# Quartered weight splits, a free pair of banks for the last turn, and moved pieces of work in a two-block transformer kernel

## Chip, core and metric

The kernel runs on one core of a Trainium2 chip. The metric is the device time of one execution in microseconds (us). Five engines work side by side, each through its own instructions in order: TensorE (PE in the profile), VectorE (DVE), ScalarE (ACT), GpSimd (POOL) and the DMA queue of SyncE (SP). They wait for each other by semaphores only.

## The reference, cut to what matters

512 positions of width 1024 go through two blocks of two layers each, all in float32.

```
first block, layer l:   x += rmsnorm(mixer_l(rmsnorm(x)))       mixer_0 = fox, mixer_1 = lru
                        x += rmsnorm(cross_attention(rmsnorm(x), rmsnorm(mem)))
                        x += rmsnorm(swiglu(rmsnorm(x)))
second block, layer l:  x = ln(a*x + 0.5*swiglu(x));  x = ln(a*x + nsa(x));  x = ln(a*x + 0.5*swiglu(x))

attention of one query tile:  s = q @ k.T + mask;  p = softmax(s);  o = p @ v;   y = concat(o) @ w_out
fox:   8 heads of 64, causal, half of the input of w_out is a gated convolution (y_b) without attention
cross: 4 heads of 256 over 256 memory rows
nsa:   8 heads of 96; three branches per head: compressed keys (31 of them), and two causal ones;
       a quarter of the input of w_out is a pooled branch (y_pool) without attention
```

## The kernel before, in words

**Weights.** Every weight matrix comes in units of up to 128x2048 numbers (a list `units`, in the order of use). A unit is loaded by SP into one of three staging buffers `STG`, cast by ACT to the matmul type into one of three `WR` buffers (`hi`, line 984), and DVE writes what the cast lost beside it (`lo`, line 1460). TensorE makes each product of three matmuls, high by high, high by low, low by high (`mm3`, lines 500 to 502). ACT and DVE have no scheduler: `after(name)` in their programs means "here cast the unit three places behind `name`". A cast waits until the buffer of the unit three places before it is dropped; a `lo` waits for its `hi`.

**Stages.** fox, cross (x0), feed-forward (f0), lru, cross (x1), f1, then f2, nsa (n0), f3, f4, nsa (n1), f5. The weight products fill most of the time. The attention of fox, x0, x1, n0 and n1 is one loop of steps, written once for each engine (`attend`) and driven by `att_steps`. An item is one or more heads of one query tile. Step i holds, in this order on TensorE: the scores of item i, the turning (transposes, `tr`, line 505) of the probabilities of item i-2, and their product with v for item i-3. DVE takes the maximum of the scores of item i (line 1567) and copies every other turned item out of PSUM (line 1480); ACT does the exponentials of item i (line 991) and the other copies (line 1071). When the last item of a query tile is through, DVE scales its output (`finish`), TensorE turns it (`turn_result`), and ACT and DVE split it into high and low parts in `HT` for the product with w_out (`ohi`, `olo`).

**Banks.** PSUM has eight banks. In fox scores go round banks 2 to 4 and turned items round 5 to 7; in cross and nsa scores go round 2 and 3, turned items and turned results round 4 and 5. The compressed scores of nsa take a bank of the same round as the scores. `pick` and `room` make TensorE wait until the former user of a bank is through. The product with w_out (`out_proj`) keeps query tile t in banks 2t and 2t+1.

**Order around the change.** `hook(i)` runs at the beginning of step i. In fox, hooks 1, 2, 5 and 6 split y_b (`ybs`: an ACT cast of 128x512, line 1183, and a DVE subtraction), hooks 4 and 8 split one whole weight unit each; in cross, hook 5 splits one; in nsa, hooks 12 and 20. In nsa the compressed branch of a query tile has four parts: `scores` (TensorE product, line 898; DVE mask and maximum; ACT exponential), `norm` (DVE), `turn` (TensorE, ACT), `out` (TensorE, line 915; DVE), placed by `nsa_hook`. The scores of the first query tile come ahead of step 0. In `out_proj` the list `first` gives the order of tiles in the first group of rows of w_out, with the last `turn_result` among them.

Of the kernel before, what the change touches and what calls it, by code (L numbers as in the profile page):

```python
# [15 lines left out]
NT = 4  # L16
# [185 lines left out]
def build(nc, T, out):  # L202
    with ExitStack() as ctx:
# [113 lines left out]
        FOX_YBS = {1: 2, 2: 3, 5: 0, 6: 1}  # L317
# [38 lines left out]
        t_banks = {"f": (5, 6, 7), "x": (4, 5), "n": (4, 5)}  # L356
        on_parts = {"f": (0, 4, F_ON), "x": (0, 8, X_ON), "n": (2, 6, N_ON)}
# [123 lines left out]
        def tensor(pe):  # L481
# [82 lines left out]

            def out_proj(s, nk, operand, points, first=range(NT), plain=False):

                names = down_units(s, nk)
                rows_of = [name[2] for name in names]
                groups = [[k] for k in rows_of[:-2]] + [rows_of[-2:]]
                for group in groups:  # L570
                    last_group = len(group) == 2
                    for t in first if group[0] == groups[0][0] else range(NT):
                        if callable(t):
                            t()
                            continue
                        if group[0] == groups[0][0]:
                            free = (ve, (s, "yfree", t)) if s in rms else (ac, (s, "sq", t))
                            room(2 * t, free)
                            room(2 * t + 1, free)
                        for k0 in group:  # L580
                            if k0 == nk - 2 and t >= 2 and not plain and s != "f5":
                                turn(s, t - 2)
                            w = take((s, "d", k0))
                            for j in range(2):
                                k = k0 + j
                                g.wait_ge(*points(k, t))
                                lh, ll = operand(k)
                                for half in range(2):
                                    c = slice(half * 512, half * 512 + 512)
                                    last = mm3(P[:, 2 * t + half, :], lh[:, tcol(t)], ll[:, tcol(t)], w[0][:, j, c],  # L590
                                               w[1][:, j, c], k == groups[0][0], k == groups[-1][-1] + 1)
                        if last_group:
                            last.then_inc(mm.sem, mm.up(s, "y", t))
                    if not last_group:
# [6 lines left out]
            def attend(s, need, values, hook=None):  # L601
# [56 lines left out]
                return lambda: turn_result(items[-1]["t"])  # L658
# [17 lines left out]
            def fox():  # L676
# [44 lines left out]
                for c in range(4):  # L721
                    w = take(("fox", "qk", c))
                    for j in range(2):
# [7 lines left out]
                         [1, 2, last_turn, 3, 0], plain=True)  # L731

            def cross(l):
# [34 lines left out]
                out_proj(s, 8, ht_operand, lambda k, t: ve.at(s, "olo", t, k // 4 * 4), [1, 0, last_turn, 2, 3])  # L768
# [41 lines left out]
            def nsa(l, prev):  # L810
# [121 lines left out]
                out_proj(s, 8, ht_operand, lambda k, t: ve.at(s, "yp", 1) if k < 2 else ve.at(s, "olo", t, 0 if k < 6 else 4),  # L932
                         [1, 3, last_turn, 2, 0])
# [42 lines left out]
        def scalar(a):  # L976
            g = Gate(a)

            def hi(n):
# [4 lines left out]
                a.copy(WR[0:p, n % NWR, 0, 0:k * w], STG[0:p, n % NSTG, 0:k * w]).then_inc(ac.sem, ac.up("hi", n))  # L984

            def after(name):
                if U[name] + 3 < len(units):
                    hi(U[name] + 3)
# [19 lines left out]
            def norm_tile(s, t, between=None, turned=None):  # L1008
# [36 lines left out]
            def down(s, nk, prepare=None, plain=False):  # L1045
# [6 lines left out]
                for t in range(NT):  # L1052
                    norm_tile(s, t, (lambda: after(names[-2])) if t == NT - 1 else None,
                              t - 1 if t in (1, 2) and not plain and s != "f5" else None)
                if plain:
                    after(names[-1])

            def attend(s, hook=None):
                items = items_of[s]()
                for i, it, b_, c_, ends in att_steps(s):  # L1060
# [22 lines left out]
                    for it in ends:  # L1083
# [3 lines left out]
                        for j0 in range(0, nk, 4):  # L1087
# [3 lines left out]
                            a.copy(HT[:, 0, k0 + j0:k0 + j0 + m, tcol(t)], ps).then_inc(ac.sem, ac.up(s, "ohi", t, j0))  # L1091

# [31 lines left out]
            def fox():  # L1124
# [51 lines left out]
                def hook(i):  # L1176
                    if i in (4, 8):
                        after(("fox", "qk", 2 if i == 4 else 3))
# [6 lines left out]
                attend("fox", hook)  # L1185
                down("fox", 8, plain=True)

            def cross(l):
# [17 lines left out]
                attend(s, lambda i: after((s, "q", 3)) if i == 5 else None)  # L1206
# [37 lines left out]
            def lru():  # L1244
# [80 lines left out]
                gates(2)  # L1325
                after(("lru", "ai", 2))
                gelu(0)
# [17 lines left out]
            def nsa(l, prev):  # L1345
# [80 lines left out]
                def hook(i):  # L1426
                    if i in (12, 20):
                        after((s, "v", 0 if i == 12 else 4))
                    for part, t in nsa_hook(i):
                        if part == "scores":  # L1430
                            scores(t)
                        if part == "turn":
                            cmp_turn(t)

                scores(ORDER["n"][0])
                attend(s, hook)
# [16 lines left out]
        def vector(v):  # L1453
            g = Gate(v)

            def lo(n):
                _, _, p, k, w = units[n]
                g.wait_ge(*ac.at("hi", n))
                cut = slice(0, k * w)
                v.tensor_tensor(WR[0:p, n % NWR, 1, cut], STG[0:p, n % NSTG, cut], WR[0:p, n % NWR, 0, cut].bitcast(F32),  # L1460
                                ALU.subtract).then_inc(ve.sem, ve.up("lo", n))

            def after(name):
                if U[name] + 3 < len(units):
                    lo(U[name] + 3)
# [34 lines left out]
            def norm_tile(s, t, between=None, turned=None):  # L1500
                if s in rms:
                    post, pre, n = rms[s]
                    if post:
# [12 lines left out]
                        if between and s not in ("fox", "lru"):  # L1516
                            between()
                    if pre:
# [25 lines left out]
            def down(s, nk, prepare=None, plain=False):  # L1544
# [6 lines left out]
                for t in range(NT):  # L1551
                    norm_tile(s, t, (lambda: after(names[-2])) if t == NT - 1 else None,
                              t - 1 if t in (1, 2) and not plain and s != "f5" else None)
                if plain:
                    after(names[-1])

            def attend(s, finish, hook=None):
                items = items_of[s]()
                for i, it, b_, c_, ends in att_steps(s):
# [10 lines left out]
                    if b_ and turned_by_vector(b_, i - 2):  # L1570
# [3 lines left out]
                        if j >= NP:  # L1574
                            g.wait_ge(*mm.at(s, "o", j - NP))
                        cp(PTB[j % NP][:, 0:kx], P[:, where[s, "t", j], 0:kx], s, "tc", j)
                    if c_ and c_["last"]:
                        finish(c_, i - 3)
                    for it in ends:
# [3 lines left out]
                        for j0 in range(0, nk, 4):  # L1583
# [4 lines left out]
                            rest(HT[:, 1, ks, tcol(t)], ps, HT[:, 0, ks, tcol(t)], s, "olo", t, j0)  # L1588

# [46 lines left out]
            def fox():  # L1636
# [61 lines left out]
                def hook(i):  # L1698
                    if i in (4, 8):
                        after(("fox", "qk", 2 if i == 4 else 3))  # L1700
# [18 lines left out]
                attend("fox", finish, hook)  # L1719
                down("fox", 8, plain=True)  # L1720

            def cross(l):
# [28 lines left out]
                attend(s, finish, lambda i: after((s, "q", 3)) if i == 5 else None)  # L1751
# [124 lines left out]
            def nsa(l, prev):  # L1876
# [152 lines left out]
                def hook(i):  # L2029
                    if i in (12, 20):  # L2030
                        after((s, "v", 0 if i == 12 else 4))
                    for part, t in nsa_hook(i):
# [4 lines left out]
                        if part == "out":  # L2037
                            cmp_out(t)

                scores(ORDER["n"][0])  # L2040
                attend(s, finish, hook)
# [70 lines left out]
```

## Time and profile before

| | |
|---|---|
| time, median of 3 runs (lowest to highest) | 3573.73 us (3573.02 to 3575.31) |
| the profiled execution: own time; span of its instructions | 3575.89 us; 3574.1 us |
| busy share of the span: PE, PEld (weight loads), DVE, ACT | 98%, 82%, 41%, 33% |
| mean granted TensorE clock, as a share of full speed | 0.994 |

The span runs from the first to the last instruction of the profiled execution; its own time is 1.8 us longer and lies 2.2 us above the median of the runs. Busy times of PE are modelled from pipelined matmuls, so what counts here is the idle time between them, with the engine and line that ended it.

### The profile page before, as it was taken

How to read it: one execution, taken by the hardware profiler on the slowest of the kernel's cores; microseconds unless marked ns; L12 is line 12 of the kernel's file. 1: busy time of each engine (PE TensorE's matmuls, PEld its weight loads, DVE VectorE, ACT ScalarE, POOL GpSimd, SP SyncE). 2: the span in 40 equal slices, each digit the busy share in tenths (PEclk: the TensorE clock that was granted, in tenths of full speed). 3: DMA queues.
4: the chain of work that ended last, by engine and by line, in shares of the span. 5: the costliest groups of instructions: out<-in, count | busy, mean ns of one | idle time of the engine just before them, and what ended most of it. 6: DMA issues, size and time to landing. Idle time of an engine off the chain costs nothing.

```text
span 3574.1 us, 39697 instructions
## 1 busy us (share of the span) xinstructions
PE 3493.7 (98%) x17605; PEld 2937.4 (82%) x17605; DVE 1460.0 (41%) x1538; ACT 1185.4 (33%) x1725; POOL 61.1 (2%) x68
## 2 busy tenths in 40 slices
PE   8999999999999999999999999999999999999999
PEld 7788788888787888888888778888888887788887
DVE  4444433337644323333335564223422345552333
ACT  3343332236633322232224343222322333432222
POOL 2000000000000000000000000000000000000000
PEclk9999999999999999999999999999999999999999
DMA  5214132223241322232322202332332223013221
GB/s 161 90 53 153 48 118 94 95 89 101 95 147 55 112 94 94 94 107 94 103 92 78 68 25 95 94 99 101 97 104 95 94 79 97 24 58 108 94 95 59
DMA packets 246333, 326.44 MB, mean 91 GB/s; under 512 B 18320, under 2 KB 215232, under 8 KB 246160
## 3 DMA queue, kind: packets, MB, share of 16 engines
q1 hardware_dynamic: 241232, 308.77, 26.7%
q0 software_dynamic: 4928, 15.12, 1.3%
q8 instruction: 138, 2.26, 0.3%
q14 instruction: 35, 0.29, 0.0%
HBM read 321.74 MB, written 2.10 MB: 91 GB/s over the span
## 4 chain that ended last, share of the span: by engine, by line
PE 89%; DVE 6%; ACT 4%; issue 0%; DMA 0%; SPq 0%; POOL 0%; DVEq 0%; ACTq 0%
PE P L500 27%; PE P L502 27%; PE P L501 27%; PE P L505 3%; PE P L653 3%; PE P L628 2%; DVE WR L1460 2%; DVE BIG L1468 1%; ACT WR L984 1%; ACT BIG L991 1%; DVE BIG L1477 1%; ACT XN L991 0%; DVE HT L1468 0%; DVE STAT L1567 0%; ACT BC L991 0%
## 5 line engine op out<-in xcount | busy, mean ns | idle before, releaser
L1460 DVE TENSOR_TENSOR WR<-STG,WR 128x2048 fp32r<-128x2048 f32 (+2 forms) x300 | 669.1, 2232 | 1356.8 <-ACT WR L984 1356.5
L500 PE MATMUL P<-HT,WR 128*128 128x512 f32 (+1 forms) x3016 | 1123.7, 373 | 5.9 <-DVE WR L1460 3.0
L501 PE MATMUL P<-HT,WR 128*128 128x512 f32 (+1 forms) x3016 | 1120.6, 372 | 0.0
L502 PE MATMUL P<-HT,WR 128*128 128x512 f32 (+1 forms) x3016 | 1120.4, 371 | 0.0
L984 ACT CAST WR<-STG 128x2048 fp32r<-128x2048 f32 (+2 forms) x300 | 557.4, 1859 | 1080.4 <-PE P L502 1080.2
L500 PEld LDWEIGHTS P<-HT,WR 128*128 128x128 f32 x3016 | 569.5, 189 | 105.0 <-DVE WR L1460 4.3
L502 PEld LDWEIGHTS P<-HT,WR 128*128 128x128 f32 x3016 | 569.4, 189 | 98.1
L501 PEld LDWEIGHTS P<-HT,WR 128*128 128x128 f32 x3016 | 569.4, 189 | 96.9
L500 PE MATMUL P<-WR,HT 128*128 128x512 f32 (+1 forms) x1344 | 525.3, 391 | 12.3 <-DVE HT L1468 12.3
L502 PE MATMUL P<-WR,HT 128*128 128x512 f32 (+1 forms) x1344 | 521.9, 388 | 0.0
L501 PE MATMUL P<-WR,HT 128*128 128x512 f32 (+1 forms) x1344 | 521.5, 388 | 0.0
L500 PEld LDWEIGHTS P<-WR,HT 128*128 128x128 f32 x1344 | 253.4, 189 | 63.1 <-DVE HT L1468 9.0
L502 PEld LDWEIGHTS P<-WR,HT 128*128 128x128 f32 x1344 | 253.0, 188 | 50.6
L501 PEld LDWEIGHTS P<-WR,HT 128*128 128x128 f32 x1344 | 253.5, 189 | 49.6
L991 ACT ACTIVATE XN<-P 128x512 f32<-128x512 f32 (+1 forms) x160 | 103.6, 651 | 554.6 <-PE P L502 554.5
L1477 DVE SCALAR_TENSOR_TENSOR BIG<-XN,P 128x512 f32<-128x512 f32 x132 | 90.7, 687 | 341.5 <-PE P L502 341.5
L628 PE MATMUL P<-BIG 128*128 128x256 f32 (+3 forms) x448 | 149.9, 441 | 7.1 <-ACT BC L991 6.8
L653 PE MATMUL P<-BIG,XN 128*128 128x96 f32 (+2 forms) x928 | 141.9, 294 | 6.2 <-DVE XN L1480 5.9
L991 ACT ACTIVATE BC<-P,STAT 128x256 f32<-128x256 f32 (+3 forms) x192 | 98.9, 520 | 109.0 <-DVE STAT L1567 108.7
L653 PEld LDWEIGHTS P<-BIG,XN 128*128 128x128 f32 x928 | 124.5, 198 | 10.1 <-DVE XN L1480 7.1
L500 PE MATMUL P<-WR,RB 128*128 128x512 f32 (+1 forms) x384 | 122.3, 334 | 0.0
L1567 DVE TENSOR_REDUCE STAT<-P 128x1 f32<-128x512 f32 (+4 forms) x142 | 83.4, 590 | 94.3 <-PE P L632 66.0
(178 smaller groups left out, 2369.6 us busy)
## 6 DMA issues: line engine op xcount, KB each, us to landing
STG<-in_w_ffn_gu_dram SPq DMA_DIRECT2D x44, 1024.0 KB, 5.1
STG<-in_ffn_w_gate_dram SPq DMA_DIRECT2D x44, 1024.0 KB, 5.3
STG<-in_ffn_w_up_dram SPq DMA_DIRECT2D x44, 1024.0 KB, 5.3
STG<-in_ffn_w_down_dram SPq DMA_DIRECT2D x44, 1024.0 KB, 4.9
STG<-in_w_ffn_down_dram SPq DMA_DIRECT2D x22, 1024.0 KB, 4.8
STG<-in_w_xkv_dram SPq DMA_DIRECT2D x16, 1024.0 KB, 5.4
STG<-in_w_in_dram SPq DMA_DIRECT2D x12, 1024.0 KB, 5.2
STG<-in_w_xq_dram SPq DMA_DIRECT2D x8, 1024.0 KB, 5.2
```

What stands on the lines that cost most here:

```text
L500: pe.matmul(o, lh, rh, start=first, stop=False)
L501: pe.matmul(o, lh, rl, start=False, stop=False)
L502: return pe.matmul(o, ll, rh, start=False, stop=last)
L505: return pe.transpose(o, i, IDENT[0:n, 0:n])
L628: last = pe.matmul(P[:, b, n * kx:(n + 1) * kx], l, r, start=j == 0, stop=j == len(qk) - 1 and a["diag"] is None)
L653: last = pe.matmul(o, PTB[j0 % NP][:, c:c + 128], c_["v"][n][j], start=j == 0, stop=j == nj - 1)
L984: a.copy(WR[0:p, n % NWR, 0, 0:k * w], STG[0:p, n % NSTG, 0:k * w]).then_inc(ac.sem, ac.up("hi", n))
L991: a.activation(o, i, f, **kw).then_inc(ac.sem, ac.up(*point))
L1460: v.tensor_tensor(WR[0:p, n % NWR, 1, cut], STG[0:p, n % NSTG, cut], WR[0:p, n % NWR, 0, cut].bitcast(F32), ALU.subtract).then_inc(ve.sem, ...
L1468: v.tensor_tensor(o, x, y, op).then_inc(ve.sem, ve.up(*point))
L1477: v.scalar_tensor_tensor(out=o, in0=x, scalar=s, in1=y, op0=op0, op1=op1).then_inc(ve.sem, ve.up(*point))
L1567: v.tensor_reduce(STAT[:, 80 + h:80 + h + nh], P[:, where[s, "s", i], 0:nh * kx].rearrange("p (h n) -> p h n", h=nh), AX.X, ALU.max, negat ...
```

## The change

- **Splits in quarters.** `hi` and `lo` can do a quarter of a unit. The whole units of hooks 4 and 8 (fox), 5 (cross), 12 and 20 (nsa) become four quarters each, at the ends of the steps listed in `SPLITS`.
- **y_b splits** of fox go to the ends of steps 3 to 6.
- **The last `turn_result`** goes to fixed banks (`last_banks`: accumulators that are free by then) and one tile product earlier in `first`.
- **nsa:** the first tile's product with the first rows of w_out (tile 3, whose operand is y_pool) goes ahead of the second to last step; the compressed scores of the first tile go from before step 0 into step 2, those of the next from step 7 to 9, and DVE's and ACT's part of all compressed scores, and DVE's `norm`, go from the beginning of a step to its end; a small product (`second(1)`) goes behind a 24-matmul one.
- **Other places:** in fox DVE copies v out of PSUM before a split instead of after it; at the end of fox and lru the last weight split goes ahead of the last tile's second norm (`middle`); in lru two gelus go ahead of a cast.

The diff, cut:

```diff
-        FOX_YBS = {1: 2, 2: 3, 5: 0, 6: 1}
+        FOX_YBS = {3: 2, 4: 3, 5: 0, 6: 1}
+        SPLITS = {"f": {7: (("qk", 2), 0), 8: (("qk", 2), 1), 9: (("qk", 2), 2), 11: (("qk", 2), 3), 12: (("qk", 3), 0),
+                        13: (("qk", 3), 1), 14: (("qk", 3), 2), 15: (("qk", 3), 3)},
+                  "x": {3: (("q", 3), 0), 4: (("q", 3), 1), 5: (("q", 3), 2), 7: (("q", 3), 3)},
+                  "n": {9: (("v", 0), 0), 10: (("v", 0), 1), 11: (("v", 0), 2), 12: (("v", 0), 3), 27: (("v", 4), 0),
+                        28: (("v", 4), 1), 29: (("v", 4), 2), 30: (("v", 4), 3)}}
+        last_banks = {"f": (1,), "x": (6, 7), "n": (0, 1)}
-            parts = {"norm": (1, 8, 24, 38), "turn": (3, 16, 32, 40), "out": (5, 20, 36, 44), "scores": (None, 7, 23, 37)}
+            parts = {"scores": (2, 9, 23, 37), "norm": (3, 10, 24, 38), "turn": (5, 16, 32, 40), "out": (7, 20, 36, 44)}
...
-                def turn_result(t):
+                def turn_result(t, banks=None):
-                        b = pick(tbank, (ve, (s, "olo", t, j0)))
+                        b = room(banks[j0 // 4], (ve, (s, "olo", t, j0))) if banks else pick(tbank, (ve, (s, "olo", t, j0)))
...
-                return lambda: turn_result(items[-1]["t"])
+                return lambda: turn_result(items[-1]["t"], last_banks[s[0]])
...
-                         [1, 2, last_turn, 3, 0], plain=True)          # fox
+                         [1, last_turn, 2, 3, 0], plain=True)
-                out_proj(... "x" ..., [1, 0, last_turn, 2, 3])
+                out_proj(... "x" ..., [1, last_turn, 0, 2, 3])
-                second(1)
                 head("k", 1, 0, "k", ve)
                 drop((s, "k", 1))
+                second(1)
...
-                scores(ORDER["n"][0])
+                    if i == len(nsa_items()) + 1:                       # in nsa's hook on TensorE
+                        out_tile(s, 8, ht_operand, points, 3, 0)
-                out_proj(s, 8, ..., [1, 3, last_turn, 2, 0])
+                out_proj(s, 8, ht_operand, points, [1, last_turn, 2, 0])
...                                                                   # scalar
+            def split_part(s, i):
+                if i in SPLITS[s[0]]:
+                    name, part = SPLITS[s[0]][i]
+                    after((s, *name), part, 4)
+                    if middle:                                          # norm_tile, between the two norms
+                        middle()
-                if plain:
-                    after(names[-1])
+                              (lambda: after(names[-1])) if plain and t == NT - 1 else None)
...
+                    split_part(s, i)                                    # end of each step of attend
+                    if tail:
+                        tail(i)
...
                 gates(2)
+                gelu(0)
                 after(("lru", "ai", 2))
-                gelu(0)
                 gelu(1)
...                                                                   # vector
+                        if s == "fox" and j == 3:
+                            g.wait_ge(*ve.at("fox", "ybs", 3))
-                after(("fox", "v", 0))
                 for t in range(NT):
                     g.wait_ge(*mm.at("fox", "v", 4))
                     cp(F_V[:, t, :], P[:, where["fox", "v", t], :], "fox", "v", t)
+                after(("fox", "v", 0))
...
-                second(1)
                 after((s, "k", 0))
                 key(2)
+                second(1)
```

## Rows read from the trace of the kernel before

**Rows 1.** The page: busy time of each engine, its share of the span, instructions.

```profile
PE 3493.7 (98%) x17605; PEld 2937.4 (82%) x17605; DVE 1460.0 (41%) x1538; ACT 1185.4 (33%) x1725; POOL 61.1 (2%) x68
```

**Rows 2.** PE's waits: for whom, us in total, times, longest.

```profile
PE P L505 <- DVE HT L1468: 14.3, 6, 3.7
PE P L500 <- DVE HT L1468: 13.9, 7, 4.4
...
PE P L628 <- ACT BC L991: 6.8, 6, 2.1
PE P L653 <- DVE XN L1480: 5.9, 5, 1.8
PE P L849 <- DVE FX L1480: 4.1, 2, 2.1
...
PE P L505 <- ACT BC L991: 2.2, 2, 1.2
```

**Rows 3.** PE's timeline: start, us, instruction, [idle before <- what ended it].

```profile
118.80 0.50 PE L500 MATMUL P<-HT,WR 128*128 128x512 f32 x1 [1.17 <-DVE BIG L1480]
...
224.43 0.50 PE L500 MATMUL P<-WR,HT 128*128 128x512 f32 x1 [1.40 <-DVE HT L1468]
...
276.80 0.58 PE L500 MATMUL P<-RB,WR 128*128 128x256 f32 x1 [2.31 <-DVE WR L1460]
...
405.20 0.47 PE L500 MATMUL P<-WR,HT 128*128 128x512 f32 x1 [1.65 <-DVE HT L1468]
...
897.74 0.77 PE L500 MATMUL P<-RB,WR 128*128 128x512 f32 x1 [3.47 <-DVE BIG L1468]
...
932.96 0.76 PE L500 MATMUL P<-WR,HT 128*128 128x512 f32 x1 [4.40 <-DVE HT L1468]
...
2024.91 1.90 PE L898 MATMUL P<-FX,BIG 96*128 96x31 f32 x16
...
2068.65 0.90 PE L505 MATMUL P<-CST,BC 128*128 128x128 f32 x3 [3.74 <-DVE HT L1468]
...
2132.73 0.66 PE L505 MATMUL P<-CST,BC 128*128 128x128 f32 x4 [2.44 <-DVE HT L1468]
...
2144.55 0.47 PE L500 MATMUL P<-WR,HT 128*128 128x512 f32 x1 [1.61 <-DVE HT L1468]
```

**Rows 4.** PE in short stretches: length, busy time, granted clock, DMA.

```profile
177.60:181.00 3.40, 1.96 (x12) 0.99 0.71 248
181.00:184.30 3.30, 3.30 (x16) 0.50 0.00 0
...
2998.90:3002.30 3.40, 1.41 (x8) 1.00 0.02 5
```

**Rows 5.** Single steps: length, then busy PE, PEld, DVE, ACT, POOL; clock.

```profile
171.96:174.31 2.35, 2.35 (x18) 1.72 (x17) 1.45 (x1) 1.35 (x2) 0.00 (x0) 1.00 0.00 0
...
366.99:368.94 1.95, 1.95 (x12) 1.61 (x10) 1.04 (x1) 0.88 (x1) 0.00 (x0) 1.00 0.00 0
...
2076.43:2078.14 1.71, 1.71 (x15) 1.35 (x13) 1.61 (x6) 1.31 (x4) 0.00 (x0) 1.00 0.00 0
```

**Rows 6.** DVE's timeline: fox steps 0, 1 and 4, n0 step 7.

```profile
163.57 0.69 DVE L1567 TENSOR_REDUCE STAT<-P 128x1 f32<-128x512 f32 x1 [0.22 <-PE P L632]
...
166.23 0.68 DVE L1567 TENSOR_REDUCE STAT<-P 128x1 f32<-128x512 f32 x1
...
172.86 2.29 DVE L1460 TENSOR_TENSOR WR<-STG,WR 128x2048 fp32r<-128x2048 f32 x1 [2.11 <-ACT WR L984]
...
2026.84 0.42 DVE L1468 TENSOR_TENSOR BIG<-P,CST 128x248 f32<-128x248 f32 x1 [2.35 <-PE P L898]
```

**Rows 7.** ACT's timeline: fox steps 1 and 4, the cast ahead of lru's gelus.

```profile
164.98 0.61 ACT L1183 CAST HT<-XN 128x512 fp32r<-128x512 f32 x1
...
170.93 1.89 ACT L984 CAST WR<-STG 128x2048 fp32r<-128x2048 f32 x1
...
893.77 1.91 ACT L984 CAST WR<-STG 128x2048 fp32r<-128x2048 f32 x1
```

More of the change, by code:

```diff
@@ L563, in first_feats, with out_groups, out_tile @@
                             drop(name)
-            def out_proj(s, nk, operand, points, first=range(NT), plain=False):
[L567 to L572, printed above, removed]
+            def out_groups(s, nk):
+                rows_of = [name[2] for name in down_units(s, nk)]
+                return [[k] for k in rows_of[:-2]] + [rows_of[-2:]]
+            def out_tile(s, nk, operand, points, t, n, plain=False):
+                groups = out_groups(s, nk)
+                if n == 0:
+                    free = (ve, (s, "yfree", t)) if s in rms else (ac, (s, "sq", t))
+                    room(2 * t, free)
+                    room(2 * t + 1, free)
+                for k0 in groups[n]:
+                    if k0 == nk - 2 and t >= 2 and not plain and s != "f5":
+                        turn(s, t - 2)
+                    w = take((s, "d", k0))
+                    for j in range(2):
+                        k = k0 + j
+                        g.wait_ge(*points(k, t))
+                        lh, ll = operand(k)
+                        for half in range(2):
+                            c = slice(half * 512, half * 512 + 512)
+                            last = mm3(P[:, 2 * t + half, :], lh[:, tcol(t)], ll[:, tcol(t)], w[0][:, j, c],
+                                       w[1][:, j, c], k == groups[0][0], k == groups[-1][-1] + 1)
+                return last
+            def out_proj(s, nk, operand, points, first=range(NT), plain=False):
+                groups = out_groups(s, nk)
+                for n, group in enumerate(groups):
+                    for t in first if n == 0 else range(NT):
                         if callable(t):
@@ L575, in out_proj @@
                             continue
[L576 to L592, printed above, removed]
+                        last = out_tile(s, nk, operand, points, t, n, plain)
+                        if n == len(groups) - 1:
                             last.then_inc(mm.sem, mm.up(s, "y", t))
-                    if not last_group:
+                    if n < len(groups) - 1:
                         last.then_inc(mm.sem, mm.up(s, "group", group[0]))
@@ L1006, in turn, with norm_tile @@
                     a.copy(HT[:, 0, ks, tcol(t)], ps).then_inc(ac.sem, ac.up(s, "hi", t, half))
-            def norm_tile(s, t, between=None, turned=None):
+            def norm_tile(s, t, between=None, turned=None, middle=None):
                 if s in rms:
@@ L1174, in fox, with tail @@
                         after(("fox", "qk", c))
-                def hook(i):
-                    if i in (4, 8):
-                        after(("fox", "qk", 2 if i == 4 else 3))
+                def tail(i):
                     if i in FOX_YBS:
@@ L1426, in hook, with tail @@
                 def hook(i):
-                    if i in (12, 20):
-                        after((s, "v", 0 if i == 12 else 4))
+                    for part, t in nsa_hook(i):
+                        if part == "turn":
+                            cmp_turn(t)
+                def tail(i):
                     for part, t in nsa_hook(i):
@@ L1498, in scaled, with norm_tile @@
                 stt(norm_buf[t % rms[s][2]], X[:, t, :], STAT[:, 8 + t:9 + t], BC[:, 1, :], ALU.mult, ALU.mult, s, "xn", t)
-            def norm_tile(s, t, between=None, turned=None):
+            def norm_tile(s, t, between=None, turned=None, middle=None):
                 if s in rms:
@@ L1517, in norm_tile @@
                             between()
+                    if middle:
+                        middle()
                     if pre:
@@ L1552, in down, with attend @@
                     norm_tile(s, t, (lambda: after(names[-2])) if t == NT - 1 else None,
[L1553 to L1557, printed above, removed]
+                              t - 1 if t in (1, 2) and not plain and s != "f5" else None,
+                              (lambda: after(names[-1])) if plain and t == NT - 1 else None)
+            def attend(s, finish, hook=None, tail=None):
                 items = items_of[s]()
@@ L1696, in fox, with tail @@
                         after(("fox", "qk", c))
-                def hook(i):
-                    if i in (4, 8):
-                        after(("fox", "qk", 2 if i == 4 else 3))
+                def tail(i):
                     if i in FOX_YBS:
@@ L1717, in finish @@
                     ve.name("fox", "on", "x", t)
-                attend("fox", finish, hook)
+                attend("fox", finish, tail=tail)
                 down("fox", 8, plain=True)
@@ L1749, in finish @@
                     ve.name(s, "on", "x", t)
-                attend(s, finish, lambda i: after((s, "q", 3)) if i == 5 else None)
+                attend(s, finish)
                 down(s, 8)
@@ L2029, in hook, with tail @@
                 def hook(i):
-                    if i in (12, 20):
-                        after((s, "v", 0 if i == 12 else 4))
+                    for part, t in nsa_hook(i):
+                        if part == "out":
+                            cmp_out(t)
+                def tail(i):
                     for part, t in nsa_hook(i):
@@ L2036, in hook @@
                             cmp_norm(t)
[L2037 to L2041, printed above, removed]
+                attend(s, finish, hook, tail)
                 down(s, 8)
```

47 lines of the change are left out of this document (26 added, 21 removed).

## The prediction

> **What bounds the kernel.** I read the page's busy times first, then PE's waits, then PE's timeline at each wait, and at last the timelines of DVE and ACT there. TensorE is busy for 3493.7 of 3574.1 us; DVE and ACT are busy for 41% and 33% [rows 1]. So the change can gain only what TensorE stands idle or runs slowly, and DVE and ACT matter only where they come late. The waits come in pairs because x0 and x1, and n0 and n1, are the same code [rows 2]. In the timeline each is one stall of 1 to 4.4 us at a known place [rows 3].
>
> There is a second loss. After the stall that ends at 179.04 TensorE had been busy for 1.96 of 3.40 us; in the next 3.30 us the granted clock is 0.50, the 1.2 GHz level, and sixteen instructions fill the stretch [rows 4]. At the 2.4 GHz level they would take half, so such a stretch costs 1.65 us. Of such stretches at 0.50, nine lie behind stalls that the change touches (one in fox, one each behind the stalls of 2.31 us at the ends of fox and lru, four in n0, two in n1). The same stall of 2.06 us was followed by 0.50 in n0 and by 1.00 in n1 [rows 2, 4], so the clock is not certain to follow.
>
> **What goes away.** Sum by the groups of [rows 2]; the parts that stay are named.
> - Scores and transposes behind the splitting of a result (14.3 us): 3.74 and 2.44 in each nsa [rows 3] go; 0.96 in each cross stays, its code is untouched. 12.4 us. In n0 the 3.74 arises because DVE waits for the cast of a whole unit, then subtracts 2.29 us, and only then comes to the result. The 2.44 is filled by the moved product of tile 3, which waits for nothing of the last attention tile.
> - First group of w_out (13.9 us): 1.40 in fox, 1.65 in x0 and x1, 1.61 and 1.60 in n0 and n1 [rows 3], 7.9 in all. There the turned last tile sits in a bank that the next tile product needs. In free banks it has one to two more products of twelve matmuls as cover. The 4.40 us of lru and 1.6 us at the start stay.
> - Scores behind an exponential (6.8 us): 1.13 and 2.12 in each nsa, 6.5 us; 0.16 in each cross stays.
> - Products behind a DVE copy (5.9 us): 1.77 in fox [rows 2], 1.81 in each cross, some 0.27 in each nsa. All behind whole units or y_b splits.
> - `second(1)` (4.1 us): 24 matmuls now lie ahead of it; what it waits for is there 2 us after the old place. Transposes behind an exponential in fox (2.2 us) go as well.
> - The last weight of fox and lru (2.31 each, 4.6 us): its ACT cast stood behind the second norm. In `middle` both halves fit while ACT would wait for DVE, and the norm that comes 0.6 us later is wanted only three products on.
> - v of fox: four copies now stand ahead of a subtraction of 2.29 us, 1.17 us [rows 3].
> - lru: the gelus go ahead of a cast of 1.91 us [rows 7], on whose other side TensorE waits 3.47 us for their bank [rows 3]. But the next stall, 4.40 us ahead of w_out, is the end of ACT's and DVE's own chain, which has the same work as before. Only ACT's own waits for TensorE in between are saved. Bounds 0 and 3.47; I take 1.5.
>
> Stalls: 12.4 + 7.9 + 6.5 + 5.9 + 4.1 + 2.2 + 4.6 + 1.2 + 1.5 = 46.3 us. With nine slow stretches of 1.65 us, 61.2 us.
>
> **What comes anew.** A quarter is a cast of 128x512 on ACT and a subtraction of 128x512 on DVE. The y_b splits have just these shapes: the cast takes 0.61 us [rows 7], and from one maximum on DVE to the next, with the exponential, the cast and the subtraction between them, pass 2.66 us [rows 6]. This loop is the price, for both engines take their work in order: the cast stands behind the exponential, which waits for the maximum, and DVE's next maximum stands behind the subtraction. TensorE's step takes 2.35 us with 512 columns in fox, 1.95 in cross, 1.71 with 384 columns [rows 5]. With fewer columns the maximum and the exponential shorten; estimates from the 0.69 us of 512 columns are 2.4 us for 384 and 2.2 for 256.
> - Cross: four quarters, each 0.2 us late; 0.8 us is less than the step or so between a copy and its use. Nothing.
> - Fox: steps 3 to 7 lose 0.3 us each (y_b splits and the first quarter), seven steps with 384 columns 0.7 each: 6.4 us late. A copy may be 1.8 us late, and step 10, which has no quarter, makes up 1.1. 3.5 us of stalls in steps 8 to 16.
> - nsa, start: TensorE now does two scores, then the compressed scores need the bank of the first: a stall of 2.0 us, for DVE's maximum stands behind the y_pool subtraction. Step 3 then waits 0.65 us for the masked scores. 2.65.
> - nsa, step 10: the compressed scores share two banks with the scores, and DVE's mask addition (the 0.42 us instruction [rows 6] that today starts right behind the product of 1.90 us [rows 3]) moves behind the maximum, the copy and a quarter of step 9. From the end of scores 9: maximum 0.65, exponential 0.8, cast 0.5, subtraction 0.7, addition 0.4, together 3.1 us; TensorE has a turning and a product, 1.3 us. It waits 1.8 us.
> - nsa, steps 10 to 12: `finish` and `norm` and quarters stand in one queue on DVE; the next copies are 1.55 and 0.65 us late. 2.2.
> - nsa, steps 27 to 30: the loop of 2.4 against 1.71 us, right behind a `finish`: 0.7 late four times, and 0.3 us was already missing there. The copies come 1.05 and 2.0 us late. 3.05.
> - nsa, steps 23 and 37: the same bank wait as in step 10 without a quarter, 0.4 each; `norm` of the last tile, now behind `finish`, makes its turning 1.15 later. 1.95.
> - nsa, end: the moved product waits 0.8 us for banks 6 and 7, which `finish` of the branch before reads; step 21 still waits 0.4 us for the result's split. 1.2.
>
> So nsa pays 12.9 us each time, fox 3.5, together 29.3. Each of these is an estimate from the rows named; its bounds are nothing (the delay fits into the step behind) and twice as much.
>
> The quarters' casts end later than the whole units did, and the loads behind them start later; the units behind are wanted only in the product with w_out or the next stage, over 50 us on, and no wait for a DMA stands in [rows 2].
>
> **A rule against a row.** The loop of 2.66 us [rows 6] says that quarters stall too. The Trainium skill, Perfetto Trace Analysis, section Optimizing Scalar/DVE Operations, says that where these engines are not saturated but cause bubbles elsewhere, breaking up instructions may let work be completed sooner; taken alone it gives the sum without the new stalls. The same section says that each instruction carries a fixed cost, some 60 ns on DVE and 93 ns on ScalarE from SBUF, so grouping helps a saturated engine: for 24 more pairs, 3.7 us as an estimate, were none hidden. No row shows a whole unit and four quarters side by side.
>
> **Sum.** 61.2 - 29.3 = 31.9 us less. The profiled execution took 3575.9 us, so 3544.0 us; the median of the runs shown is 2.2 us lower: 3542 us, 0.9% faster. Its own range is 3530 to 3550.
>
> **Rivals.**
> 1. *The quarters hide.* The new stalls fade, since a late engine makes up in each step without extra work: 29.3 us more gained, 3513 us. For it: DVE and ACT are busy less than half of a step [rows 5]. Against: it is the loop, not the busy time, that is longer than the step. By the rule on breaking up this is the case.
> 2. *The clock follows the new stalls.* The 2.0 us at the start, those of 1.8 and 1.55 us in steps 10 to 12, and the 2.0 us behind step 30 of each nsa, with those of fox, each bring a stretch at 0.50: seven times 1.65 us, 3554 us. For it: 1.77 us behind 1.2 us did so in fox [rows 2, 4]. Against: 1.65 us did not.
> 3. *The stalls move on.* TensorE reaches the next wait sooner and stands there, as I expect for lru; were it so for the casts and results too, 3567 us or more, no change.
> 4. *Slower.* The quarters lie open: each shows its 1.3 us of cast and subtraction, 32 times (41.6 us), the eight compressed scores each stall as in step 10 (14.4 us), and the nine slow stretches come back (14.9 us). That is 70.9 against 61.2: 3583 us. The case is decided when new stalls exceed 61 us, twice what I count.
>
> **How the numbers follow.** Forecast 0.55, rival 1 0.2, rival 2 0.15, rival 3 0.05, rival 4 0.05. The low end, 3514, is rival 1 and the high end, 3562, lies beyond rival 2; below and above is left out some 0.15. Of no change I speak within 0.2%, 7.1 us. Rivals 1 and 2 and the forecast are faster, 0.9; rival 3 is mostly within, 0.06; slower 0.04.
>
> **What would show it.** In the profile after, the stalls of 1.40, 1.65 and 1.61 us at w_out, 2.31 us at the memory keys, and 2.06 us at `second(1)` must be gone; 3.74 us must be 0.4. In lru the 3.47 us must be 1.4 and the 4.40 us larger. New stalls must stand before the scores of nsa step 10, before a product with v in fox steps 8 to 16, and in nsa at step 32 or just before. The prediction is wrong if none of these new stalls is there (then 3513), if they carry the slow clock, or if the DVE timeline shows subtractions of quarters that start long after their cast.

## The result, and the profile after

The changed kernel takes 3550.36 us (median of four runs, 3549.34 to 3551.95) against 3573.57 us before on the same chip (3573.02 to 3575.31): ratio 0.9935, 95% interval 0.9917 to 0.9952. The forecast was 3542 us, with 3530 to 3550 as its own range and 3514 to 3562 as the whole one: the measured time lies 0.4 us above the first and inside the second. The gain is 23 us where 32 were forecast.

The page of the changed kernel, busy time of each engine, answering [rows 1]:

```profile
span 3547.7 us, 39728 instructions
...
PE 3485.3 (98%) x17605; PEld 2929.2 (83%) x17605; DVE 1462.1 (41%) x1562; ACT 1187.2 (33%) x1749; POOL 61.1 (2%) x68
```

The span is 26.4 us shorter (3574.1 to 3547.7). These two lines already split it: PE's busy time fell by 8.4 us (3493.7 to 3485.3) for the same 17605 instructions, for the most part by the clock, as the stretches below show, and its idle time (span less busy) from 80.4 to 62.4 us, by 18.0. The other 24 instructions on DVE and on ACT, three more for each of eight units, cost 2.1 and 1.8 us of busy time in all.

PE's waits of the changed kernel (for whom, us in total, times, longest), answering [rows 2]. Lines moved: weight products are now 506 to 508, transposes 511, scores 641, products with v 666, compressed scores 911.

```profile
PE P L511 <- DVE XN L1505: 9.6, 2, 9.1
PE P L666 <- DVE XN L1508: 9.3, 11, 1.7
PE P L511 <- DVE XN L1508: 6.9, 4, 1.8
PE P L506 <- ACT WR L999: 6.6, 1, 6.6
PE P L641 <- DVE BIG L1496: 5.9, 8, 1.8
PE P L911 <- ACT BC L1012: 3.7, 2, 1.8
...
PE P L511 <- DVE HT L1496: 2.9, 4, 1.0
...
PE P L506 <- ACT XN L1012: 1.7, 1, 1.7
PE P L506 <- DVE HT L1496: 1.6, 1, 1.6
```

What was to go is gone. Splits of results ahead of transposes fell from 14.3 to 2.9 us (0.96 in each cross and 0.48 in each nsa are left), those ahead of w_out from 13.9 to 1.6 (the start of the kernel; the 4.4 us of lru are now in the row of 6.6), `second(1)` from 4.1 us to nothing. In their place stand waits that are new or have grown: copies ahead of products with v (5.9 to 9.3, eleven times), copies ahead of transposes (6.9), DVE's mask addition ahead of scores (5.9), an exponential ahead of the compressed scores (3.7), and the wait at the end of lru, 6.6 us instead of 4.4. The profile puts this one down to a cast of ACT, which ends at 918.79; the first result of lru that the product reads is finished by DVE at 918.80, and the last experiment bears out that it is this one.

PE's timeline of the changed kernel at the largest of them (start, us, instruction, idle before and what ended it): two in lru, then n0 at its start, in steps 10 and 12, behind step 30, in step 40 and at its end.

```profile
883.09 0.47 PE L506 MATMUL P<-RB,WR 128*128 128x512 f32 x1 [1.69 <-ACT XN L1012]
...
918.94 0.77 PE L506 MATMUL P<-WR,HT 128*128 128x512 f32 x1 [6.60 <-ACT WR L999]
...
1983.09 0.63 PE L911 MATMUL P<-FX,BIG 96*128 96x31 f32 x4 [1.84 <-ACT BC L1012]
...
2010.83 0.70 PE L641 MATMUL P<-BIG 128*128 128x512 f32 x1 [1.84 <-DVE BIG L1496]
...
2018.65 0.57 PE L666 MATMUL P<-BIG,XN 128*128 128x96 f32 x3 [1.69 <-DVE XN L1508]
...
2066.42 0.62 PE L511 MATMUL P<-CST,BIG 128*31 128x128 f32 x4 [1.75 <-DVE XN L1508]
...
2092.63 0.62 PE L511 MATMUL P<-CST,BIG 128*31 128x128 f32 x4 [1.67 <-DVE XN L1508]
...
2108.58 0.51 PE L506 MATMUL P<-WR,HT 128*128 128x512 f32 x1 [0.84 <-DVE BIG L1496]
```

In n1 these stalls are the same within 0.05 us. PE in short stretches behind such stalls in the changed kernel (start and end, length, busy time, granted clock, DMA):

```profile
1985.00:1988.40 3.40, 3.15 (x9) 0.50 0.00 0
2012.60:2016.00 3.40, 3.40 (x24) 1.00 0.02 5
...
2066.40:2069.80 3.40, 3.38 (x24) 1.00 0.91 297
2092.60:2096.00 3.40, 3.37 (x32) 1.00 0.02 5
3002.10:3005.50 3.40, 3.40 (x13) 0.51 0.00 0
3005.50:3008.90 3.40, 3.15 (x9) 0.50 0.00 0
...
3039.70:3043.10 3.40, 3.40 (x16) 0.50 0.00 0
```

Between the first and the last stages the kernel before has twelve stretches of some 3.4 us at the 1.2 GHz level: one in fox, one in lru behind its first stall, two ahead of w_out in lru, one each at the ends of fox and lru, four in n0 and two in n1. The changed one has six: the two at lru's w_out, which were there before, and the four that these rows show, behind new stalls of nsa.

### The profile page after: what moved, and what is told of

It is laid out like the page before. It is cut to its first block, busy times and chain, and to the rows that moved or that the text cites. A ratio compares the mean times of both kernels' runs of the same rounds, so it can differ in the third digit from the quotient of the medians.

```text
span 3547.7 us, 39728 instructions
## 1 busy us (share of the span) xinstructions
PE 3485.3 (98%) x17605; PEld 2929.2 (83%) x17605; DVE 1462.1 (41%) x1562; ACT 1187.2 (33%) x1749; POOL 61.1 (2%) x68
## 3 DMA queue, kind: packets, MB, share of 16 engines
q1 hardware_dynamic: 241232, 308.77, 26.4%
## 4 chain that ended last, share of the span: by engine, by line
PE 91%; DVE 4%; ACT 4%; issue 0%; DMA 0%; SPq 0%; DVEq 0%; ACTq 0%
PE P L506 28%; PE P L508 28%; PE P L507 28%; PE P L511 3%; PE P L641 2%; PE P L666 2%; DVE WR L1483 1%; ACT WR L999 1%; DVE STAT L1596 1%; ACT BIG L1012 1%; ACT BC L1012 1%; DVE BIG L1496 1%; PE P L928 0%; PE P L911 0%; DVE BIG L1505 0%; ACT L1012 0%
## 5 line engine op out<-in xcount | busy, mean ns | idle before, releaser
L1483 DVE TENSOR_TENSOR WR<-STG,WR 128x2048 fp32r<-128x2048 f32 (+3 forms) x324 | 672.8, 2079 | 1359.5 <-ACT WR L999 1359.2
L999 ACT CAST WR<-STG 128x2048 fp32r<-128x2048 f32 (+3 forms) x324 | 561.7, 1735 | 1073.0 <-PE P L508 1072.8
```

The source lines that it names most:

```text
L999: a.copy(WR[0:p, n % NWR, 0, cut], STG[0:p, n % NSTG, cut]).then_inc(ac.sem, ac.up("hi", n, *((part,) if part < of - 1 else ())))
```

## The experiments

Each kernel was timed beside the kernel before on the same chip, on three chips in all (medians of the kernel before: 3572.4, 3573.5 and 3574.0 us). The first four test the two theories on what is left: the loop of quarters, and the moved compressed scores.

**Quarters, the subtraction a step later.** ACT's cast stays where it is; DVE subtracts the quarter in the step behind.

```diff
 # vector
-                if i in SPLITS[s[0]]:
-                    name, part = SPLITS[s[0]][i]
+                if i - 1 in SPLITS[s[0]]:
+                    name, part = SPLITS[s[0]][i - 1]
```

> The changed kernel, with DVE's subtraction of each quarter one step later than ACT's cast of it. The work is the same. Theory 1 (the new stalls come from the loop maximum, exponential, cast, subtraction, maximum, which is longer than TensorE's step): without the wait inside the step the loop is gone. The four stalls in fox (3.2 us) fall under 0.5, the stall of 1.84 us before the scores of nsa step 10 falls to about 0.5, those at steps 30 to 32 (0.86 and 1.75 us) mostly go, the 1.69 us at step 12 stays, because finish and norm stand in the queue there. 9 to 12 us less than the changed kernel, about 3539. Rival (the extra instructions and their work on ACT and DVE are what delays, whatever their order): the stalls stay, time within 3 us of 3550.

3534.17 us (ratio 0.9891, 0.9876 to 0.9906): 16.2 us below the changed kernel, where 9 to 12 were expected. DVE's timeline in fox of the changed kernel (start, us, instruction, idle before):

```profile
178.83 0.69 DVE L1483 TENSOR_TENSOR WR<-STG,WR 128x512 fp32r<-128x512 f32 x1 [0.75 <-ACT WR L999]
179.44 0.55 DVE L1596 TENSOR_REDUCE STAT<-P 128x1 f32<-128x384 f32 x1
181.24 0.69 DVE L1483 TENSOR_TENSOR WR<-STG,WR 128x512 fp32r<-128x512 f32 x1 [1.25 <-ACT WR L999]
181.84 0.55 DVE L1596 TENSOR_REDUCE STAT<-P 128x1 f32<-128x384 f32 x1
182.31 0.68 DVE L1508 COPY XN<-P 128x512 f32<-128x512 f32 x1
183.64 0.69 DVE L1483 TENSOR_TENSOR WR<-STG,WR 128x512 fp32r<-128x512 f32 x1 [0.65 <-ACT WR L999]
```

The same timeline of this kernel:

```profile
179.84 0.56 DVE L1596 TENSOR_REDUCE STAT<-P 128x1 f32<-128x384 f32 x1 [0.51 <-PE P L645]
180.31 0.68 DVE L1508 COPY XN<-P 128x512 f32<-128x512 f32 x1
180.91 0.68 DVE L1483 TENSOR_TENSOR WR<-STG,WR 128x512 fp32r<-128x512 f32 x1
181.88 0.56 DVE L1596 TENSOR_REDUCE STAT<-P 128x1 f32<-128x384 f32 x1 [0.29 <-PE P L645]
```

In the changed kernel the subtractions come every 2.40 us, the loop of maximum, exponential, cast and subtraction, and DVE stands idle ahead of each until the cast is there, up to 1.25 us. A step later the cast is done when DVE arrives: the subtraction follows the copy at once, and what DVE waits for is PE's next scores. Of fox's stalls (0.47, 0.69, 1.20, 0.80) only 0.47 is left; in n0 step 10 falls from 1.84 to 0.40 and the three behind step 27 (0.28, 0.86, 1.75) become 0.28. With the same instructions on every engine 11.8 us of idle time (62.4 to 50.6) were due to the wait of one engine for the other inside a step. Another 2.7 us is PE's busy time (3485.3 to 3482.6), and it is not the clock: as many stretches at the 1.2 GHz level are left, six. The rest lies between the profiled executions and the medians.

**Compressed scores at their old places and steps.**

```diff
-            parts = {"scores": (2, 9, 23, 37), "norm": (3, 10, 24, 38), "turn": (5, ...
+            parts = {"norm": (1, 8, 24, 38), "turn": (3, ...), "out": (5, ...), "scores": (None, 7, 23, 37)}
+                scores(ORDER["n"][0])            # ahead of step 0, each engine
-                attend(s, hook, tail)            # ACT and DVE: all parts in hook again
+                attend(s, hook)
```

> The changed kernel with the compressed scores and norm of nsa back where they were (first scores ahead of step 0, the others at the beginnings of steps 7, 23, 37, norm at 1, 8, 24, 38); quarters, banks and the rest as changed. Theory 1 (a bank shared with the scores is given back late because the mask addition now stands behind the maximum): the stalls of 1.85, 1.84, 0.46 and 0.40 us go, 1.13 and 0.43 us come back at the start, the turning at step 40 waits 0.5 instead of 1.7 us. About 4 us less in each nsa, and the slow clock behind the stalls of steps 2 and 10 (up to 3 stretches of 1.7 us) may go too: 3537 to 3543. Rival (the move pays: DVE no longer stands idle for TensorE's product at the beginning of a step): 3550 or slower.

3529.64 us (0.9877, 0.9861 to 0.9894), better than either theory had it. n0's stalls fall from 12.9 to 7.2 us: 1.13 and 0.43 at the start for 1.84 and 0.25, nothing at the bank of step 10 for 1.84, 0.32 in step 12 for 1.69, 0.52 in step 40 for 1.67. PE's waits show it (in the changed kernel: 9.3 for products with v, 6.9 for transposes, 5.9 for the mask addition, 3.7 for the compressed scores; the last two are gone):

```profile
PE P L666 <- DVE XN L1507: 7.1, 12, 1.2
...
PE P L511 <- DVE XN L1507: 4.6, 4, 1.8
...
PE P L641 <- ACT BC L1013: 2.6, 4, 1.1
```

PE is busy for 3477.5 us, 7.8 less than in the changed kernel. No stretch at 1.2 GHz is left in nsa, as the attention of n0 shows (n1 is the same):

```profile
1980.00:2110.00 130.00, 122.69 (x876) 1.00 0.08 25
```

So moving the scores cost 20.7 us by itself, about a third of it in the clock (four stretches of 1.65 us).

**Both.**

> Both edits together: subtraction one step later, compressed scores back. Theory 1: the two add except for the stall of 1.84 us before step 10, which both remove: 3527 to 3534. Rival (one queue delay is behind both, whichever order): no better than the better one alone.

3518.66 us (0.9847, 0.9833 to 0.9862), below the 3527 to 3534 expected. Together the edits gain 31.7 us where the single gains sum to 36.9; the stall before step 10, which either edit removes, is part of the difference. The largest stalls of each nsa are 1.13 us at the start and 0.85 at the end; PE is busy for 3474.5 us.

**Only the scores' steps moved.** New step numbers, but ACT's and DVE's parts at the beginning of the step.

```diff
-                def tail(i):                     # ACT and DVE in nsa
-                    for part, t in nsa_hook(i):
-                attend(s, hook, tail)
+                attend(s, hook)                  # all parts in hook
```

> The changed kernel with its new steps for the compressed branch (first scores in step 2, next in step 9), but ACT's and DVE's parts at the beginning of a step as before. Tells apart which half of the move costs. Theory 1 (the place within the step: the mask addition behind maximum, copy and quarter): the stalls of 1.84, 0.46 and 0.40 us before scores go and the turning at step 40 waits 0.5 us, the 1.85 us at the start stays; 3534 to 3540. Rival (the other step is what costs): near 3550.

3537.24 us (0.9895, 0.9879 to 0.9912). Of the 20.7 us, some 13.1 are thus the move from beginning to end of a step, 7.6 the move to other steps, if they are undone in this order; the old steps with the parts at their ends were not run. The 1.84 us at the start stays, as it goes with the steps; the 1.84 at step 10 is gone, since the mask addition no longer stands behind the quarter.

**Three parts undone, each alone.** Whole units and y_b splits at their old places; the banks, the orders of `first` and the moved product as before; `second(1)`, `middle`, v of fox and lru's gelus as before.

```diff
-        FOX_YBS = {3: 2, 4: 3, 5: 0, 6: 1}
+        FOX_YBS = {1: 2, 2: 3, 5: 0, 6: 1}
+        SPLITS = {"f": {4: ("qk", 2), 8: ("qk", 3)}, "x": {5: ("q", 3)}, "n": {12: ("v", 0), 20: ("v", 4)}}
```

> The changed kernel with the whole units and the y_b splits back at the beginnings of their old steps (fox 1, 2, 5, 6 and 4, 8; cross 5; nsa 12, 20); compressed scores, banks and the rest as changed. Theory 1: fox gets back 4 us of stalls and a slow stretch for 3.2 us of stalls, cross 1.8 us each, nsa some 2.1 and 3.7 us and slow stretches for about 6 us of stalls: 8 to 14 us more, 3558 to 3564. Rival (quarters are worth nothing, being paid back by new stalls): within 3 us of 3550.

```diff
-                return lambda: turn_result(items[-1]["t"], last_banks[s[0]])
+                return lambda: turn_result(items[-1]["t"])
...                                               # and the old orders of first
-                    if i == len(nsa_items()) + 1:
-                        out_tile(s, 8, ht_operand, points, 3, 0)
```

> The changed kernel with the last turn in the old round of banks, one tile later, and the moved product of tile 3 back in its old place. Theory 1 (these are plain stalls of TensorE that free banks and the moved product remove): 1.40 us in fox, 1.65 in each cross, 2.44 and 1.61 for 0.85 in each nsa come back, 11.1 us, and the slow clock behind the 2.44 us in up to two places (3.4 us): 3561 to 3565. Rival (the stalls only move to the next group of w_out, since the same splits must be through): within 4 us of 3550.

```diff
-                              (lambda: after(names[-1])) if plain and t == NT - 1 else None)
+                if plain:
+                    after(names[-1])
...
+                second(1)                        # ahead of the 24 matmuls, and so on
```

> The changed kernel with the other moves undone: second product of nsa, last weight of fox and lru behind the second norm, v of fox behind the subtraction, gelus behind the cast. Theory 1: 1.17 + 2 x 2.31 + 2 x 2.06 us of stalls and 1.5 us in lru come back, 11.4 us, and three slow stretches of 1.65 us: 3562 to 3567. Rival (what is saved there is lost at the next wait): within 4 us of 3550.

3558.22 us (0.9960, 0.9945 to 0.9975), 3563.81 (0.9971, 0.9959 to 0.9982) and 3565.83 (0.9977, 0.9967 to 0.9986): the three parts are worth 7.9, 13.5 and 15.5 us, each within the range expected. The stalls are back with their sizes: with the old banks 1.40 us in fox, 1.65 in each cross, 2.44 and 1.60 in each nsa; with the other moves undone 1.18, 2.31 and 2.32, and 4.1 for both `second(1)`. With the scores' -20.7 the parts sum to 16.1 us and not to 23.2, so they do not simply add. In the profiled executions the sum is 19.6 of 26.4 us, and 4.0 of the 6.8 that are missing lie in PE's busy time (4.4 of 8.4), where the clock counts.

PE's waits of the kernel with whole units (lines four less than in the changed one):

```profile
PE P L507 <- DVE HT L1490: 9.4, 4, 3.7
PE P L662 <- DVE XN L1502: 8.1, 7, 1.8
...
PE P L637 <- ACT BC L1007: 4.6, 4, 2.1
```

The 3.74 and the 2.12 us of nsa are back and the 1.81 of each cross, as the prediction had them. But n0's stalls sum to 13.5 us with whole units and to 12.9 with quarters: in nsa, as written, quarters only spread the stall. They paid in cross, where nothing came in place of 1.81 us, and in fox (4.3 to 3.2 us of stalls, and none of the slow clock that follows 1.78 us there with whole units: 6.83 us at 0.50). Yet in cross too DVE waits for each cast, and the subtractions come 2.16 us apart, against TensorE's step of 1.95 [rows 5]:

```profile
355.75 0.69 DVE L1483 TENSOR_TENSOR WR<-STG,WR 128x512 fp32r<-128x512 f32 x1 [0.81 <-ACT WR L999]
...
357.91 0.69 DVE L1483 TENSOR_TENSOR WR<-STG,WR 128x512 fp32r<-128x512 f32 x1 [1.14 <-ACT WR L999]
```

That is the 0.2 us late, four times, which the prediction called less than the way from a copy to its use; no stall came of it.

**The end of lru.** On the kernel with the late subtraction and the old scores, the gelus behind the cast again:

```diff
-                gelu(0)
                 after(("lru", "ai", 2))
+                gelu(0)
```

> The kernel with DVE's quarters a step later and the compressed scores at their old places, and in lru the two gelus behind the weight cast again, as before the change. My theory: the stall ahead of lru's gelu product returns from 1.7 to about 3.5 us, and the stall ahead of w_out shrinks from 6.6 to about 4.8, for ACT and DVE end lru's chain at the same time either way; the move of the gelus gained nothing much. The sum of the two is about 8.3 us in both kernels; 3518 to 3521 us. Rival: the move does gain what it takes from the first stall, then the stall ahead of w_out stays at 6.6 us and the sum is 10.1: 3521 to 3524 us. The stalls in the trace decide, since 2 us is less than the times can tell.

3519.55 us (0.9854, 0.9837 to 0.9870). PE's timeline in lru without this edit:

```profile
880.21 0.47 PE L506 MATMUL P<-RB,WR 128*128 128x512 f32 x1 [1.69 <-ACT XN L1013]
...
916.07 0.76 PE L506 MATMUL P<-WR,HT 128*128 128x512 f32 x1 [6.61 <-ACT WR L1000]
```

And with it:

```profile
880.24 0.77 PE L506 MATMUL P<-RB,WR 128*128 128x512 f32 x1 [3.46 <-DVE BIG L1495]
...
915.38 0.77 PE L506 MATMUL P<-WR,HT 128*128 128x512 f32 x1 [4.39 <-DVE HT L1495]
```

The two stalls sum to 8.3 us with the gelus ahead and to 7.85 with them behind: the whole 1.77 us moved to the next wait, and 0.45 more. It is the same pair as 3.47 and 4.40 before [rows 3]. The 0.45 us go with the clock. Behind the 3.46 us PE runs slowly here, and at full clock behind 1.69 us. In the kernel above with the other moves undone the gelus are behind the cast too, and there the stall of 3.46 us was not followed by the slow clock. Its two stalls and the stretch behind the first come first here; the last row is the stretch behind the first stall in the kernel of this experiment:

```profile
889.14 0.47 PE L506 MATMUL P<-RB,WR 128*128 128x512 f32 x1 [3.46 <-DVE BIG L1497]
...
923.18 0.77 PE L506 MATMUL P<-WR,HT 128*128 128x512 f32 x1 [4.80 <-DVE HT L1497]
...
889.10:892.50 3.40, 3.36 (x15) 1.00 0.08 8
...
880.20:883.60 3.40, 3.36 (x8) 0.52 0.08 7
```

From the beginning of the first stall to w_out pass 37.5 us in that kernel (923.18 - 889.14 + 3.46) and 37.5 with the gelus ahead (916.07 - 880.21 + 1.69), but 38.6 where the slow stretch lies between (915.38 - 880.24 + 3.46). So the move of the gelus takes nothing from the chain; the 1.1 us that it can gain is the slow stretch behind the first stall.

So the order at the end of that chain was changed instead: results 0 and 1 of lru go ahead of the last weight split, DVE's outputs and ACT's last gelu.

```diff
+                result(1)                        # ACT, ahead of gelu(3)
-                for i in range(1, NK):
+                for i in range(2, NK):
+                result(0)                        # DVE, ahead of the outputs and the weight split
+                result(1)
-                result(0)
-                for i in range(1, NK):
+                for i in range(2, NK):
```

> Subtraction one step later and compressed scores back (3518.7 us by itself), and in lru the first two results ahead of a weight subtraction and of the gelu outputs on DVE, and ahead of the last gelus on ACT. Theory 1 (the stall of 6.6 us ahead of w_out is DVE's queue: after the last scan it subtracts 2.3 us and multiplies 1.2 us before the first result): the stall falls to about 3.0 us and half of the slow 6.8 us behind it goes: 3513 to 3516. Rival (the chain of exponentials and scans itself ends then, or the results behind become late): 3517 to 3520.

3514.75 us (0.9833, 0.9818 to 0.9848), the fastest version, 35.6 us below the changed kernel. PE's timeline ahead of lru's w_out:

```profile
912.26 0.47 PE L506 MATMUL P<-WR,HT 128*128 128x512 f32 x1 [3.21 <-DVE HT L1496]
```

The 6.61 us become 3.21, for w_out needs results 0 and 1 first, and its first operand now comes ahead of work that can wait.

## Why the prediction was right, and where it was off

**The size of the miss.** Measured 3550.4, forecast 3542: 8.4 us, so that rival 2 with 3554 us came nearer than the forecast. Of the 14.9 us taken off for the clock 8.4 are found in PE's busy time. Of the 6.5 that are missing, 5.0 are three stretches of 1.65 us; the other 1.5 is busy time that came anew, for which the kernel with the late subtraction, with six stretches too and 2.7 us less busy, points to the loop of the quarters. Stalls come out 1.0 better (17.0 and 18.0), and some 3 lie in the profiled executions, of which that of before was 2.3 us above its median and that of after 0.9 below.

**What goes away: right.** Every stall named is gone or at its foretold rest: 1.17, 1.40, 1.65, 1.61, 2.31, `second(1)`; 3.74 is 0.48 where 0.4 was said. Without lru I took 44.8 us; 47.3 went (18.0 net, 28.9 that came anew by the table below, 0.4 that lru lost). Of the 2.5 us more, 1.9 are two waits of each nsa that the sum did not name, 0.43 us in the first steps and 0.52 at step 40.

**What comes anew: right in place and nearly in size.** The table compares the terms of the prediction with PE's timeline.

| | predicted | measured |
|---|---|---|
| fox | 3.5 | 0.47 + 0.69 + 1.20 + 0.80 = 3.2 |
| nsa, start | 2.65 | 1.84 + 0.25 = 2.1 |
| step 10 | 1.8 | 1.84 |
| steps 10 to 12 | 2.2 | 1.69 + 0.52 = 2.2 |
| steps 27 to 32 | 3.05 | 0.28 + 0.86 + 1.75 = 2.9 |
| steps 23 and 37, turning at 40 | 1.95 | 0.46 + 0.40 + 1.67 = 2.5 |
| end, step 21 | 1.2 | 0.84 + 0.48 = 1.3 |
| one nsa | 12.9 | 12.9 in n0, 12.8 in n1 |

The loop was the mechanism, as the 2.40 us from one subtraction to the next show; the prediction had estimated 2.4 for 384 columns. That it is the loop and not the engines' load is shown by the kernel with the subtraction a step later. In step 10 the queue behind the quarter was right too: 1.84 us fell to 0.40 with whole units in other steps, and to 0.40 with the subtraction late.

**The failed term: nine slow stretches of 1.65 us that vanish.** The prediction took off 14.9 us for the clock and let the new stalls run at full clock. Ten stretches did vanish, one more than counted (behind lru's first stall, now 1.69 us), but four came anew behind the new stalls of nsa; net six, 9.9 us by the prediction's own price, 8.4 in PE's busy time. That is rival 2 in part: it had seven, and 3554 us. It had the starts of n0 and n1 right, and one in steps 10 to 12, in n1 alone; fox brought none, nor did step 30. That new stalls carry the slow clock was also one of the signs by which the prediction said that it would be wrong. The prediction itself had noted that the clock is not certain to follow, and then gave the new stalls no share of that in its sum.

**lru: stalls wrong in sign, small.** I took a gain of 1.5 us between bounds of 0 and 3.47; the sum of both stalls grew from 7.87 to 8.29. The reason given for caution, that the second stall is the end of ACT's and DVE's own chain, was the answer: the two kernels with the gelus behind the cast show it. What lru gained is the clock behind its first stall, a stretch that the prediction had not counted.

**A misreading, without a term in the sum.** Rival 1 was supported with DVE and ACT being busy for less than half of a step. In the three steps of [rows 5] DVE is busy for 1.45 of 2.35, 1.04 of 1.95 and 1.61 of 1.71 us and ACT for 1.35, 0.88 and 1.31: more than half in all but one.

**The rule on breaking up.** The rows show all three outcomes of the same quarters: in cross 1.81 us gone for nothing, in nsa as written 13.5 us against 12.9, and with the subtraction a step later 8.3. The Trainium skill, Perfetto Trace Analysis, section Optimizing Scalar/DVE Operations, says that breaking up may let work be completed sooner where engines that are not saturated cause bubbles; the runs agree in cross, in part in fox, and in nsa only with the subtraction a step later. The same section's fixed cost per instruction (about 60 ns on DVE, 93 on ScalarE from SBUF) is of the size that the pages show: 2.1 us and 1.8 us for 24 more instructions, 88 and 75 ns each.

**Not settled.** Why the clock follows one stall and not another of the same length. No experiment here was made for that.

## What to carry to other kernels

Cutting a long instruction into pieces that fit a step can make a loop with another engine that is longer than the step. Where few such steps follow each other the delay may be hidden, as in cross; where it is not, as in nsa, give the second half of a hand-over (here cast, then subtraction) to the next step. When a stall is removed, look whether the next one ends the same chain of other engines; if so, shorten that chain or reorder its end, for earlier work ahead of it only moves the stall. When work is moved to the end of a step, count all that then stands between it and the engine that waits, and charge new stalls with the same clock that is credited to the old ones.

## What the runs showed of the hardware beyond this

The granted clock does not go by the length of a stall alone. In the changed kernel 1.84 us at the start of n0 was followed by 0.50, and 1.84 us in step 10 by 1.00. The stall of 1.67 us in step 40 of n0 was followed by 1.00 there (2092.60 in the rows above), and in the kernel with the late subtraction by 0.51, as this stretch of its PE shows:

```profile
2083.70:2087.10 3.40, 3.40 (x19) 0.51 0.02 5
```

The matmuls ahead of that stall are the same in both kernels; one difference is that in the changed kernel stalls of 0.86 and 1.75 us end some 31 and 26 us earlier, and in the other one neither is there. Whether that matters no run here decides.
